# Two feed-forward layers by seven block products: differences, low parts, first group and input scaling rearranged

## The reference

```python
def half_ffn(x, g, w_up, w_down):
    a, b = jnp.split(rmsnorm(x, g) @ w_up, 2, axis=-1)
    return x + 0.5 * ((jax.nn.silu(a) * b) @ w_down)
# x = half_ffn(x, ffn1);  x = x + token mixing (attention, mLSTM);  x = half_ffn(x, ffn2);  final norm
```

## Time and profile before

| | us |
|---|---|
| median of 3 runs | 2905.01 (2901.2 to 2907.52) |
| profiled execution, its own time | 2902.4 |
| span of the profiled execution | 2900.6 |
| TensorE busy | 2612.0 (90%) |
| VectorE, GpSimd, ScalarE busy | 1892.7, 1414.0, 1118.1 |

### The profile page before, as it was taken

The page is one execution under the profiler, slowest core; times in us unless marked ns, Lnnn a source line. Parts: engine busy times, 40 slices in busy tenths (PEclk is TensorE's granted clock), DMA queues, the critical chain, the costliest instruction groups (busy, mean ns, idle before and its releaser), DMA issues. The chain is left out here.

```text
span 2900.6 us, 46871 instructions
## 1 busy us (share of the span) xinstructions
PE 2612.0 (90%) x17420; PEld 2526.9 (87%) x17420; DVE 1892.7 (65%) x3147; ACT 1118.1 (39%) x2170; POOL 1414.0 (49%) x998
## 2 busy tenths in 40 slices
PE   5999998899999899999998989987899997899998
PEld 4888897889889798999987869987888896898888
DVE  7766667776676445998635634238676668766665
ACT  4433333333334342212547753224333333333333
POOL 4755666766565411212223114327566667666563
PEclk7999999999999999999999999998999999999999
DMA  3312222122221331213332413312222221222221
GB/s 125 102 64 83 73 88 66 66 88 88 73 74 45 124 87 55 76 31 95 103 91 62 64 52 121 133 51 73 71 76 80 81 88 52 81 88 73 73 88 73
DMA packets 214946, 230.38 MB, mean 79 GB/s; under 512 B 35196, under 2 KB 192952, under 8 KB 214592
## 3 DMA queue, kind: packets, MB, share of 16 engines
q1 hardware_dynamic: 214720, 227.37, 25.0%
HBM read 200.14 MB, written 25.99 MB: 78 GB/s over the span
## 5 line engine op out<-in xcount | busy, mean ns | idle before, releaser
L458 PE MATMUL f1ps<-f1xs_lo,f1w_hi 128*128 128x288 f32 x1232 | 368.8, 299 | 33.9 <-POOL f1xs_lo L452 24.9
L458 PE MATMUL f2ps<-f2xs_lo,f2w_hi 128*128 128x288 f32 x1232 | 369.1, 300 | 32.8 <-POOL f2xs_lo L452 25.0
L678 POOL TENSOR_TENSOR f2w_lo<-f2raw,f2w_hi 128x512 fp32r<-128x512 f32 x220 | 311.8, 1417 | 134.8 <-ACT f2w_hi L591 125.4
L678 POOL TENSOR_TENSOR f1w_lo<-f1raw,f1w_hi 128x512 fp32r<-128x512 f32 x220 | 310.6, 1412 | 128.9 <-ACT f1w_hi L591 120.2
L459 PE MATMUL f2ps<-f2xs_hi,f2w_lo 128*128 128x288 f32 x1232 | 366.7, 298 | 0.0
L459 PE MATMUL f1ps<-f1xs_hi,f1w_lo 128*128 128x288 f32 x1232 | 366.0, 297 | 0.0
L460 PE MATMUL f2ps<-f2xs_hi,f2w_hi 128*128 128x288 f32 x1232 | 365.6, 297 | 0.0
L460 PE MATMUL f1ps<-f1xs_hi,f1w_hi 128*128 128x288 f32 x1232 | 364.9, 296 | 0.0
L678 POOL TENSOR_TENSOR f1w_lo<-f1ts,f1w_hi 128x512 fp32r<-128x512 f32 x176 | 242.3, 1376 | 191.2 <-ACT f1w_hi L591 184.7
L678 POOL TENSOR_TENSOR f2w_lo<-f2ts,f2w_hi 128x512 fp32r<-128x512 f32 x176 | 242.5, 1378 | 188.8 <-ACT f2w_hi L591 182.0
L458 PE MATMUL d_ps<-xn_lo,d_w_hi 128*128 128x384 f32 x864 | 298.1, 345 | 6.3 <-POOL xn_lo L297 4.6
(11 more groups left out here) (384 smaller groups left out, 7104.0 us busy)
## 6 DMA issues: line engine op xcount, KB each, us to landing
f1raw<-in_w_ffn_up SPq DMA_DIRECT2D x44, 1024.0 KB, 5.1
f2raw<-in_w_ffn_up SPq DMA_DIRECT2D x44, 1024.0 KB, 5.1
f1raw<-in_w_ffn_down SPq DMA_DIRECT2D x22, 1024.0 KB, 4.8
f2raw<-in_w_ffn_down SPq DMA_DIRECT2D x22, 1024.0 KB, 4.9
d_raw<-in_w_in SPq DMA_DIRECT2D x35, 512.0 KB, 5.2
p_dram<-stage SPq DMA_DIRECT2D x24, 576.0 KB, 3.4
b_sg<-p_dram SPq DMA_DIRECT2D x16, 576.0 KB, 4.9
x_dram<-xT SPq DMA_DIRECT2D x1, 4608.0 KB, 15.2
```

Of the source, the lines that this page charges most:

```text
L458: nc.tensor.matmul(out, w_hi, x_lo, start=first, stop=False)
L678: nc.gpsimd.tensor_tensor(slot(w_lo, j), source(j), slot(w_hi, j).bitcast(F32), ALU.subtract)\
```

## The change

- **Weight differences one per block product.** `ahead` is gone; `weight_term(q)` makes one difference, at steps from the table `TERMS_AT`: for the next a tile at b0, b2, b3 and d3, for the next b tile at d5, d7, a0 and a2.
- **Low parts of the gated product on GpSimd.** `hidden_lo` moves from VectorE to GpSimd, at 1, 3 (two of them) and 5 steps after the b tile's last step, behind that step's `split_lo`. Readers wait on the same semaphore `hl_ok`.
- **Plain products in each half's first group.** The tiles a0 and b0 of each half have 8 steps (4 outputs, 2 depths) in place of 7. They need only A and B (now both quarters of A, so 8 operands), no weight differences and no adds: silu reads PSUM, and the multiply has one operand in PSUM. Each has 4 weight blocks for 8 steps.
- **Input scaled from PSUM.** The copy `rb` is gone: `apply` reads the spread rows in PSUM. The diagonals are made for one half at a time, 5 each; the second half's come at step `EDGE`, and their spread stands in TensorE's queue before step `EDGE + 1`. In the first half the four `ta` buffers lie in memory that is free then; the sums S are made at steps 0, 2, 4, 6 of a0, in place; they are needed from step a1 m = 2. In the second half `apply` comes at EDGE + 1, 3, 7, 11 and `combine` at EDGE + 5, 9, 14, 17.
- The ring of weight blocks has 7 slots in place of 9.

The core of the diff ("..." marks what is left out):

```diff
-    def rows(self, act):
-        for x in range(4):
-            act.wait_ge(self.spread_ok, x + 1)
-            self.nc.scalar.activation(self.rb[:, x * QT:(x + 1) * QT], self.ps[x], ACT.Copy).then_inc(self.rb_ok, 1)
...
-            self.nc.vector.scalar_tensor_tensor(self.ta[k % 2][:, half], self.xT[:, c, tok], self.gain[:, c:c + 1],
-                                                self.rb[:, tok], ALU.mult, ALU.mult).then_inc(self.xa_ok, 1)
+            self.nc.vector.scalar_tensor_tensor(quarters(self.ta[h][k][:, half]),
+                                                quarters(self.xT[:, c, h * HT:(h + 1) * HT]), self.gain[:, c:c + 1],
+                                                self.ps[h], ALU.mult, ALU.mult).then_inc(self.xa_ok, 1)
...
+        if h == 0:
+            dve.wait_ge(self.al_ok, n + 1)
+            dve.wait_ge(self.bl_ok, n + 1)
+        elif k:
+            dve.wait_ge(self.sl_p, 2 + min(k, 2))
...
-    RING, RAWS, TS = 9, 3, 4
+    RING, RAWS, TS = 7, 3, 4
...
+    TERMS_AT = {}
+    for q in range(4 * len(UP)):
+        j, back = COMBO[UP[q // 4]], {"a": (6, 4, 5, 4), "b": (5, 3, 3, 4)}[UP[q // 4][1]][q % 4]
+        TERMS_AT.setdefault(LAST[j + (2, 2, 3, 6)[q % 4] - RING] - back, []).append(q)
...
+    A_AT, S_AT = [(0, 0, 0, 0), (EDGE + 1, EDGE + 3, EDGE + 7, EDGE + 11)], [(0, 2, 4, 6), tuple(EDGE + e for e in (5, 9, 14, 17))]
...
             @block.gpsimd
+                def hidden_lo(h, g, x):
+                    G = group(h, g)
+                    pool.wait_ge(hh_ok, nth(G, x))
+                    nc.gpsimd.tensor_tensor(hidden(h_lo, h, g, x), product(x), hidden(h_hi, h, g, x).bitcast(F32),
+                                            ALU.subtract).then_inc(hl_ok, 1)
+                    pool.wait_ge(hl_ok, nth(G, x))
+                def rest(s):
+                    for back, places in ((1, (0,)), (3, (1, 2)), (5, (3,))):
+                        h, kind, g, m = STEPS[s - back] if s >= back else STEPS[0]
+                        if kind == "b" and m == (6 if g else 7):
+                            for x in places:
+                                hidden_lo(h, g, x if g else PLAIN_X[x])
...
             @block.vector
-                    if s in FREED:
-                        ahead(FREED[s])
...
+                    for q in TERMS_AT.get(s, ()):
+                        weight_term(q)
+                    if s == EDGE:
+                        dve.wait_ge(hm_ok, 4 * NG)
+                        norm.diagonals(dve, 1)
...
             @block.tensor
+                def up_plain(s, h, kind, m):
+                    o, d = divmod(m, 2)
+                    j = COMBO[h, kind, 0] + 2 * (o // 2) + d
+                    pe.wait_ge(lo_ok, j + 1)
+                    if d == 0:
+                        free_bank(s)
+                    hi, lo, x = slot(w_hi, j), slot(w_lo, j), ((0, 1), (7, 2))[o % 2][d]
+                    for k in range(4):
+                        if kind == "a" and m < 2:
+                            pe.wait_ge(norm.bl_ok if d else norm.al_ok, 4 * h + k + 1)
+                        last = product3(nc, bank(s), hi[:, k], lo[:, k], xs_hi[:, x, k], xs_lo[:, x, k],
+                                        d == 0 and k == 0, d == 1 and k == 3)
+                    last.then_inc(mm_ok, 1)
...
-                norm.spread(pe)
+                norm.spread(pe, 0)
                 for s, (h, kind, g, m) in enumerate(STEPS):
+                    if s == EDGE + 1:
+                        pe.wait_ge(ad_ok, added(NG - 1, "b", 7))
+                        norm.spread(pe, 1)
```

More of the change, by code:

```diff
@@ L340, with __init__ @@
 class HalfNorm:
[L349 removed]
+    def __init__(self, nc, sem, K, xT, gain, xs_hi, xs_lo, diag, ta, st, ps, ps_sums):
         self.nc, self.K, self.xT, self.gain, self.xs_hi, self.xs_lo = nc, K, xT, gain, xs_hi, xs_lo
[L351 to L354, removed]
+        self.diag, self.ta, self.st, self.ps, self.ps_sums = diag, ta, st, ps, ps_sums
+        (self.sums_ok, self.mean_ok, self.inv_ok, self.root_ok, self.diag_ok, self.spread_ok, self.xa_ok,
+         self.s_ok, self.ah_ok, self.bh_ok, self.sh_ok, self.al_ok, self.bl_ok, self.sl_p, self.sl_v) = (
+             sem("n_" + n) for n in ("sums", "mean", "inv", "root", "diag", "spread", "xa", "s", "ah", "bh", "sh", "al",
+                                     "bl", "slp", "slv"))
     def sums(self, pe):
@@ L471, in ffn, with plain @@
     sem = lambda n: ctx.enter_context(nc.semaphore(tag + n))
-    RING, RAWS, TS = 9, 3, 4
+    RING, RAWS, TS = 7, 3, 4
     ORDER = [tile for g in range(NG) for tile in (("a", g), ("b", g), ("d", g - 1)) if tile[1] >= 0] + [("d", NG - 1)]
     TILES = [(h, kind, g) for h in range(2) for kind, g in ORDER]
-    COMBO, STEP, STEPS, LAST = {}, {}, [], []
+    COMBO, STEP, STEPS, LAST, USE = {}, {}, [], [], {}
+    def plain(tile):
+        return tile[1] != "d" and tile[2] == 0
     for tile in TILES:
[L477 to L482, removed]
@@ L483, in ffn @@
-    UP = [tile for tile in TILES if tile[1] != "d"]
+        at = len(STEPS)
+        COMBO[tile], STEP[tile] = len(LAST), at
+        LAST += [at + m for m in ((1, 3, 5, 7) if tile[1] == "d" else (2, 3, 6, 7) if plain(tile) else range(7))]
+        STEPS += [tile + (m,) for m in range(8 if tile[1] == "d" or plain(tile) else 7)]
+    for s, step in enumerate(STEPS):
+        if step[1] != "d":
+            USE[s] = USE[s - 1] if plain(step) and step[3] % 2 else len(set(USE.values()))
+    ENDS = {u: s for s, u in USE.items()}
@@ L484, in ffn @@
+    UP = [tile for tile in TILES if tile[1] != "d" and not plain(tile)]
     DOWN = [tile for tile in TILES if tile[1] == "d"]
-    OWNER = [(tile, x) for tile in TILES for x in range(4 if tile[1] == "d" else 7)]
+    OWNER = [(tile, x) for tile in TILES for x in range(4 if tile[1] == "d" or plain(tile) else 7)]
     FREED = {LAST[j - RING]: j for j in range(RING, len(LAST))}
-    UPS = [s for s, step in enumerate(STEPS) if step[1] != "d"]
-    OPERAND = [0, 1, 4, 5, 3, 6, 2]
+    OPERAND = [0, 1, 3, 4, 6, 5, 2]
@@ L515, in ffn @@
                              "dn_ev", "sq_ok", "sum_ok"))
-        norm = HalfNorm(nc, sem, K, xT, gain, xs_hi, xs_lo, rb, diag, (ta0, ta1), st,
-                        [ps[:, 4 + x, 0:QT] for x in range(4)], None if summed else ps[:, 0, 0:NT])
+        norm = HalfNorm(nc, sem, K, xT, gain, xs_hi, xs_lo, diag, [ta, [ta[k % 2] for k in range(4)]], st,
+                        [ps[:, 4:6, 0:QT], ps[:, 2:4, 0:QT]], None if summed else ps[:, 0, 0:NT])
+        assert USE[STEP[1, "a", 0]] % 4 == 0
         up_v = w_up[0].rearrange("(k p) n -> p k n", p=P)
@@ L552, in source @@
                 return raw[:, n % RAWS].rearrange("p (f n) -> p f n", f=FG)[:, :, x * 2 * P:(x + 1) * 2 * P]
+            if plain(tile):
+                return part(n, x % 2, x // 2)
             if x in TERM:
@@ L586, in split_hi @@
                     weights_in(act, tile)
-                    if tile[1] != "d" and x in TERM:
+                    if tile[1] != "d" and not plain(tile) and x in TERM:
                         act.wait_ge(t_ok, term(tile, TERM[x]) + 1)
@@ L652, in rest @@
                             norm.high(act, 1, k, "B")
-                        if r == 3:
-                            norm.high(act, 1, k, "S")
+                        for h in range(2):
+                            if s == S_AT[h][k] + 1 - h:
+                                norm.high(act, h, k, "S")
                     if s >= len(STEPS) - 16:
@@ L659, in _ @@
                 norm.root(act)
-                norm.rows(act)
                 for k in range(4):
-                    if k < 2:
-                        split_hi(k)
-                    for which in "ABS":
-                        norm.high(act, 0, k, which)
-                for j in range(2, RING):
+                    norm.high(act, 0, k, "A")
+                    norm.high(act, 0, k, "B")
+                    split_hi(k)
+                for j in range(4, RING):
                     split_hi(j)
@@ L766, in evict @@
                         return
+                    if g == 0:
+                        if kind == "b" and m % 2:
+                            multiply(G, s, PLAIN_X[m // 2])
+                        return
                     if m:
```

289 lines of the change are left out of this document (142 added, 147 removed).

## The result

| | before | changed |
|---|---|---|
| median | 2904.56 us (4 runs beside the changed kernel) | 2672.27 us (4 runs, 2671.97 to 2672.65) |
| profiled execution, its own time and span | 2902.4, 2900.6 | 2672.19, 2670.4 |
| ratio, 95% interval | | 0.9201 [0.9185, 0.9217] |

The changed kernel is 232 us faster. 2665 was forecast, with a range of 2635 to 2728.

The account below looks back on a forecast made before the run. TensorE's own work, waits (mainly for late VectorE evictions) and low-clock time bound the kernel. Per FFN 94.1 - 3 + 18 + 11 = 120, twice 240, off 2902.4 gives 2662, plus 2.6 for the median: 2665 us, range 2635 to 2728.

Parts of the forecast that it names:

- The repeating groups: Repeating groups of both FFNs: d2's eviction stalls and the clock drop go, saving 94.1 us, less 3, per FFN.
- the remainder of 3: Repeating groups: 3 us per FFN taken back for small remainders such as d4's late eviction, range 0 to 18.
- GpSimd's low parts at nothing: Repeating groups: four low parts moved to GpSimd, 3.5 us a group, costed at nothing under some 7 us of cover.
- The start: Each FFN up to d0: d0 starts at about 86 instead of 104.3; 18 us saved, bounds 8 to 24.
- VectorE's arrears: First tiles of an FFN: VectorE's sums, some 10 us in arrears, cost 1.5 us for a late multiply or add.
- The boundary: Between an FFN's halves: 10.1 us lost against 24.2, 3.2 for two extra steps; 11 saved, bounds 2 and 17.
- the one drop: Boundary: TensorE's wait of about 3.3 us before the spread may drop the clock once, costing 1.7 us.
- Edges give nothing: Rival: only the repeating groups gain; arrears and diagonals replace what leaves the edges; 2723 us, chance 0.13.
- The port is the bound: Rival: the port GpSimd and VectorE share limits; half of the 3.55 stays per group; 2724 us, chance 0.14.
- what would show it: Profile signs: boundary-only DVE waits near 10 us, group 35.2, clock 1.00, spread differences, d0 near 86, boundary stage near 50.
- signs of being wrong: TensorE waiting for `w_lo` each group, eviction waits of about 2 us staying, or EDGE + 1 spread waiting over 6.

## Why the prediction was right, and where its sizes were off

- **The repeating groups** (94.1 less 3 per FFN). Right, and shown: bringing both edits back brings the stall of 3.55 and the low clock back; the edits alone in the kernel before give 183.3 where the sum had 182. In the changed kernel the remainder of 3 isn't there: only 1.5 us are lost, once, in the first down tile, so the term is 92.6. VectorE's timeline shows where the eight differences of a group went. Seven are shown (the eighth is at d3): first those at d5, d7, a0, a2 and b0, where TensorE waits for nothing, then the two at b2 and b3, which are all that is left in the stretch b2 to d0:

```profile
204.69 0.68 DVE L769 TENSOR_TENSOR f1ts<-f1raw 128x512 f32<-128x512 f32 x1
...
207.88 0.68 DVE L769 TENSOR_TENSOR f1ts<-f1raw,f1ts 128x512 f32<-128x512 f32 x1
208.65 1.61 DVE L769 TENSOR_TENSOR f1ts<-f1raw 128x512 f32<-128x512 f32 x1
...
212.37 0.97 DVE L769 TENSOR_TENSOR f1ts<-f1raw,f1ts 128x512 f32<-128x512 f32 x1
...
218.77 0.71 DVE L769 TENSOR_TENSOR f1ts<-f1raw 128x512 f32<-128x512 f32 x1
...
223.57 1.14 DVE L769 TENSOR_TENSOR f1ts<-f1raw,f1ts 128x512 f32<-128x512 f32 x1
...
225.17 1.25 DVE L769 TENSOR_TENSOR f1ts<-f1raw 128x512 f32<-128x512 f32 x1
```

- **GpSimd's low parts at nothing.** Right within the groups. They take 828 ns each, where 0.88 us was taken, and the experiment with one extra for each shows that 3.5 us more a group would also have been covered there. At the boundary they were not free, as the term of the boundary shows. The 7 slots cost no wait for weights: the one wait for `w_lo` in f1, 4.9 us, is at the FFN's first step.
- **The start** (18). 17.5: d0 at 86.8, forecast 86, before 104.3. VectorE's arrears do hold two banks back, for 2.11 and 1.07 us; the sum had 1.5 for both. That d0 is only 0.8 late has some luck in it: counted back from d0, the first three steps were over at about 40.3, where 41 was taken. No run undoes the plain products, the scaling from PSUM or the 7 slots alone, so how the gain divides among them is not shown.
- **The boundary** (11). 6.0: this is the term that was mis-sized. The 16 steps lose 15.0 us, not 10.1, and with the same accounting as before (24.2 lost, and 3.2 to pay for the two extra steps of the second half's first group) 24.2 - 15.0 - 3.2 = 6.0 is saved. By parts: the wait for eviction and diagonals 2.1 (forecast 3.3; five diagonals took 1.62, not 2.5); the spread 1.2 (1); the wait for the eviction of EDGE + 6 5.45 (2.0), for that of EDGE + 10 2.33 (2.1); the lower clock 3.9 (1.7), which is what TensorE's 30.73 busy us hold beyond 16 steps at 1.60 and the spread. Two things were missing in the step: the first `combine` waits 2.0 us for a low part of the gated product which the change itself had moved to GpSimd, behind the input's low parts; and a sum beside GpSimd costs 1.40 to 1.65, not the mean of 0.95 from the earlier trace rows, a mean over sums with and without GpSimd beside them. The clock fell elsewhere too: not behind the spread's wait of 2.09, where the one drop was put (it reads 1.00 in 405 to 422 us), but behind the 5.45 and again behind the 2.33. The price of a sum was to be had from the profile of before, which showed one of 1.55 at this place, behind a wait of `combine` for a GpSimd low part, though of the input and not of the product.

The sum as measured: 92.6 + 17.5 + 6.0 = 116.1 an FFN, 232 in all, which is the 232 measured. The forecast had 120. The boundary's 5 too many would have put it 10 us off in two FFNs; it is only 7 off because the 3 taken back in the groups were 1.5 too many the other way, which is luck.

**The rivals.** "Edges give nothing" fell by experiment: from 2718.9 to 2672.3 the other edits give 47, as do start and boundary by the windows (2 x 23.5). "The port is the bound" fell with the windows: nothing is lost in the groups. The Trainium skill's page "Perfetto Trace Analysis", section "Optimizing Scalar/DVE Operations", warns that moving work between VectorE and GpSimd might not help, as they share a read port; here it does help, the four low parts back on VectorE cost 38.7 us. Where GpSimd was made the bound, the exclusive lock of the Trainium skill's page "SBUF — State Buffer", section "SBUF: two separate sides", would have a group take 18 x 1.29 + 16 x 0.79 + 8 x 0.68 + 4 x 0.45 = 43.1 us, an estimate with that page's rule from unhindered rows; 41.8 was measured, 3% less than such a lock would need, so the trace agrees nearly but not in full. In the changed kernel what the two engines cost each other shows in the time at the edges, where TensorE waits behind sums of 1.40 to 1.65 us.

Of what would show it, all came but two: one of the three waits for an eviction (1.49 us at 91.62) is in the first down tile and not at the boundary, and the boundary's stage is 55.0, not near 50 (61.0 - 6.0, the two extra steps counted in). Of the signs of being wrong, one came, taken at its word: waits for evictions of about 2 us stay (2.33, and one of 5.45), but at the boundary and not in the groups.

## What to carry to other kernels

Two edits that relieve one chain don't add up: find how late the chain is, and what each takes off it; the first is worth most (142 to 153 of 191 us here), and the second only what is left of the lateness. Price an operation at a crowded place by the rows with the same neighbours, not by the mean of its group. When work changes engines, look for who waits for its last piece, above all where the pattern ends: there the queue of the new engine is another one, and the cover that the repeating part gives is gone.

## What the runs showed of the hardware

- Short stalls don't lower TensorE's granted clock here: with 0.74 and 0.65 us in every group it reads 1.00; with 3.55 in every group it reads 0.95 to 0.97, at a further cost of 1.7 us a group on average. But the length of one wait doesn't decide. The wait of 2.09 before the boundary's spread is followed by full speed in the changed kernel (1.00 in 405 to 422 us), and by matmuls 0.24 us apart in the version with the later low part. In the kernel before, most stalls of 3.55 are followed by the low clock, but the one before 315.81 is not:

```profile
315.81 0.37 PE L458 MATMUL f1ps<-f1h_lo,f1w_hi 128*128 128x288 f32 x1 [3.56 <-DVE xT L765]
316.02 0.29 PE L459 MATMUL f1ps<-f1h_hi,f1w_lo 128*128 128x288 f32 x1
316.15 0.29 PE L460 MATMUL f1ps<-f1h_hi,f1w_hi 128*128 128x288 f32 x1
```

  What else decides, these runs don't show.

- VectorE's operations with both operands in SBUF stretch beside GpSimd (a 128x288 sum 0.46 alone, 1.40 to 1.65 beside; a 128x512 difference 0.68 and 1.61). Those with one operand in PSUM do not. All adds and evictions of f1 in the changed kernel, with their shortest, median and longest time in ns:

```profile
L782 DVE TENSOR_TENSOR f1ev<-f1ev,f1ps x280: 440/455/457, 71.7 to 810.2; 128x288 f32<-128x288 f32 x140
L807 DVE SCALAR_TENSOR_TENSOR xT<-f1ps,xT x176: 741/758/758, 90.7 to 835.7; 128x576 f32<-128x576 f32 x176
```

  Nor do the diagonals much, with one operand in SBUF: five in 1.62 us (0.32 each, 0.28 in the earlier trace rows), and for half of that GpSimd made a low part of 0.79.
